# Opening of a fused two-block kernel: modulation rows loaded and summed whole, one group of four depth blocks multiplied in fp32 unsplit, two phases of 4 and 12 depth blocks, a short lead

## What is computed

```python
c_act = jax.nn.silu(c)                                  # c: 2048 values
mod = (c_act @ ada_w[i] + ada_b[i])[:, None, :]         # ada_w[i]: 2048 x 6144
shift, scale, gate = jnp.split(mod, 3, axis=-1)
h = rmsnorm(x, norm_g[i]) * (1.0 + scale) + shift
proj = h @ ret_w_in                                     # 2048 x 12288: q, k, v, g
```

## Time and profile before

| | us |
|---|---|
| three runs | 2258.05 (2257.55 to 2258.37) |
| the profiled execution | 2258.34 |
| its span | 2256.6 |
| TensorE busy | 2213.6 (98%) |
| DVE busy | 1489.8 (66%) |
| ACT busy | 1039.2 (46%) |
| mean granted clock of TensorE | 0.993 |
| HBM read | 498.04 MB, 222 GB/s over the span |

### The profile page before, as it was taken

How to read it: one execution, slowest core, us unless ns; L and a number is a source line. 1 busy time by engine, 2 the same in 40 slices (tenths; PEclk the granted TensorE clock), 3 DMA queues, 4 the chain that set the end, 5 groups by cost and what they waited for, 6 DMA issues and landing times.

```text
span 2256.6 us, 26895 instructions
## 1 busy us (share of the span) xinstructions
PE 2213.6 (98%) x10348; PEld 1835.5 (81%) x10348; DVE 1489.8 (66%) x1899; ACT 1039.2 (46%) x1353; POOL 101.7 (5%) x81
## 2 busy tenths in 40 slices
PE   5999999999999989999999999999999999999999
PEld 4878887878887778989888788878888888888887
DVE  7898778778876978655685555665555455555554
ACT  4544354443444445445455455454444344344343
POOL 0000000000000000000021200000100000000000
PEclk8999999999999999999999999999999999999999
DMA  9998577878887759735466454555566665666654
GB/s 349 374 329 300 169 265 270 308 251 311 286 299 249 280 200 338 247 109 173 148 188 218 155 177 139 167 190 187 185 189 186 195 187 186 196 186 189 194 186 141
DMA packets 139794, 501.91 MB, mean 222 GB/s; under 512 B 15633, under 2 KB 16145, under 8 KB 139153
## 3 DMA queue, kind: packets, MB, share of 16 engines
q1 hardware_dynamic: 139376, 499.99, 66.2%
q10 hardware_dynamic: 290, 0.21, 0.0%
HBM read 498.04 MB, written 2.10 MB: 222 GB/s over the span
## 4 chain that ended last, share of the span: by engine, by line
PE 88%; DVE 5%; DMA 3%; ACT 2%; issue 1%; POOL 1%; SPq 0%; DVEq 0%; ACTq 0%
PE ps L1008 72%; PE ps L1019 7%; PE ps L1080 2%; PE ps L1033 2%; DMA raw<-in_ret_in 2%; DVE wlo L1569 1%; ACT whi L1259 1%; DVE raw L1576 1%; DMA arena<-in_ret_in 1%; PE ps L1072 0%; DVE arena L1776 0%; PE ps L1177 0%; DVE x L1784 0%; POOL arena L1981 0%; DVE alo L1569 0%
## 5 line engine op out<-in xcount | busy, mean ns | idle before, releaser
L1569 DVE TENSOR_TENSOR wlo<-raw,whi 128x1024 fp32r<-128x1024 f32 (+1 forms) x711 | 867.9, 1226 | 575.9 <-ACT whi L1259 573.4
L1259 ACT ACTIVATE whi<-raw 128x1024 fp32r<-128x1024 f32 (+1 forms) x711 | 739.6, 1044 | 802.8 <-PE ps L1008 639.5
L1008 PE MATMUL ps<-whi,ahi 128*128 128x512 f32 x2482 | 789.3, 398 | 4.6 <-ACT whi L1259 1.7
L1008 PE MATMUL ps<-wlo,ahi 128*128 128x512 f32 x2482 | 771.8, 391 | 5.3 <-DVE wlo L1569 5.2
L1008 PE MATMUL ps<-whi,alo 128*128 128x512 f32 x2482 | 771.8, 391 | 0.0
L1008 PEld LDWEIGHTS ps<-wlo,ahi 128*128 128x128 f32 x2482 | 466.7, 188 | 107.2 <-DVE wlo L1569 8.2
L1008 PEld LDWEIGHTS ps<-whi,alo 128*128 128x128 f32 x2482 | 467.5, 188 | 98.9
L1008 PEld LDWEIGHTS ps<-whi,ahi 128*128 128x128 f32 x2482 | 457.0, 189 | 96.9 <-issue 3.8
L1576 DVE SCALAR_TENSOR_TENSOR raw<-raw,arena 128x1024 f32<-128x1024 f32 x184 | 223.9, 1218 | 0.0
L1019 PE MATMUL ps<-whi,ahi 128*128 128x512 f32 x254 | 99.6, 392 | 0.0
L1019 PE MATMUL ps<-wlo,ahi 128*128 128x512 f32 x254 | 98.9, 389 | 0.0
(11 more groups left out here) (209 smaller groups left out, 1343.8 us busy)
## 6 DMA issues: line engine op xcount, KB each, us to landing
raw<-in_mlp SPq DMA_DIRECT2D x256, 512.0 KB, 3.6
raw<-in_ret_in SPq DMA_DIRECT2D x188, 512.0 KB, 4.9
raw<-in_ada_t SPq DMA_DIRECT2D x184, 512.0 KB, 5.0
raw<-in_in SPq DMA_DIRECT2D x80, 512.0 KB, 4.3
raw<-in_ret_out SPq DMA_DIRECT2D x64, 512.0 KB, 4.9
raw<-in_mla_in SPq DMA_DIRECT2D x48, 512.0 KB, 4.6
raw<-in_mla_out SPq DMA_DIRECT2D x32, 512.0 KB, 4.2
raw<-in_out SPq DMA_DIRECT2D x32, 512.0 KB, 3.8
```

Of the source, the lines that this page charges most:

```text
L1008: mm = e.matmul(acc_[:, :], (ahi, alo, ahi)[m][:, slot, kb, tb * P:(tb + 1) * P], parts[m][:, chunk(n)], start=first and m == 0, stop=False)
L1259: e.activation(high(i)[:, 0:ncol], raw_of(n)[:, 0:ncol], ACT.Copy).then_inc(*s_hi.up(i))
L1569: e.tensor_tensor(low(i)[:, 0:ncol], raw_of(n)[:, 0:ncol], high(i)[:, 0:ncol].bitcast(F32), ALU.subtract).then_inc(*s_lo.up(i))
```

## The change

1. Ada rows: one load of 1 MB (2048 inputs, two neighbouring lanes) and one DVE instruction with its sum per tile, in place of two; `mods` and `gate_sum` lose the addition of the halves. The stored array is laid out so that a partition's row is 8 KB in one piece.
2. `DIRECT`: the four blocks with index 0, 2, 4, 6 (qk of depth blocks 0 to 3) aren't split. TensorE multiplies the raw fp32 weight by the modulated input in `scr`, one fp32 product in place of three. Their lanes are free when TensorE has used them.
3. Phases of 4 and 12 depth blocks. The rows of depth blocks 4 to 15 (24 loads of 1 MB) are strewn from index 8 to index 38. v next stays in PSUM from the first phase into the second.
4. `pump` emits loads as far ahead as before, but splits and sums (`make`) only two blocks ahead of TensorE until index 44, then seven as before.
5. Turns 0 to 3 come before the first block, turns 4 to 7 after index 8 and the next ones. The diagonal comes ahead of the first ada sums. The low part of h0 is made after the split of the v block of its depth block.
6. Gate rows and the second layer's rows are placed only after every second weight, so that pairs of lanes stay aligned.

```diff
-PHASES = [range(0, 4), range(4, 10), range(10, 16)]
+PHASES = [range(0, 4), range(4, 16)]
+BESIDE, LAZY = 8, 44
+DIRECT = range(0, BESIDE, 2)
-ORDERS = [("qk", "v", "g", "qk next", "v next"), ("v next", "qk next", "g", "v", "qk"),
-          ("qk", "v", "qk next", "v next", "g")]
+ORDERS = [("qk", "v", "g", "qk next", "v next"), ("v next", "qk", "v", "qk next", "g")]
...
-    for kbs, first_w, last_w in ((PHASES[1], 8, 30), (PHASES[2], 30, 60)):
-        for j in range(24):
-            due.setdefault(first_w + j * (last_w - first_w) // 24, []).append((kbs[j // 4], j // 2 % 2, j % 2))
+    for j in range(24):
+        due.setdefault(BESIDE + j * 16 // 24 * 2, []).append((PHASES[1][j // 2], j % 2))
...
+    def pump(upto, made=None):
+        while at["next"] < len(plan) and at["weight"] <= upto:
+            n = at["next"]
+            at["next"] += 1
+            do("load", n)
+            at["weight"] += plan[n][0] == "w"
+        if made is None:
+            made = upto if at["used"] > LAZY else min(upto, at["used"] + 2)
+        consume(made)
+    def make():
+        n = at["made"]
+        at["made"] += 1
+        if plan[n][0] == "w":
+            i = at["split"]
+            at["split"] += 1
+            if i not in DIRECT:
+                do("split", i, n)
+            if i < BESIDE and i % 2:
+                do("mod_low", range(i // 2, i // 2 + 1))
+            return
+        _, layer, kb, c = plan[n]
+        do("adt", layer, kb, c, n)
+        if c == 1 and layer == 0 and kb in PHASES[0]:
+            do("mods", layer, kb, 1)
+            if kb:
+                mod_begin(range(kb, kb + 1))
...
-    pump(0, 3)
+    pump(7, -1)
     do("norm_diag", "h0")
-    pump(0, 6)
+    for _ in range(2):
+        make()
     turn_first(0)
-    mod_to(0)
     turn_first(1)
+    mod_begin(range(1))
+    consume(1)
+    turn_first(2)
+    turn_first(3)
...
+            def direct(name, kb, i, got, first, end):
+                n = weights[i]
+                w.wait_ge(*s_raw[lanes[n]].on(n))
+                w.wait_ge(*s_act.on(("mod_first", kb)))
+                for c, tb in got:
+                    acc_ = empty(got[c, tb]) if first else ps[got[c, tb][0]]
+                    mm = e.matmul(acc_[:, :], scr[:, kb % 4 * 256 + tb * P:kb % 4 * 256 + (tb + 1) * P], raw_of(n)[:, chunk(c)], start=first, stop=end)
```

More of the change, by code:

```diff
@@ L176, in schedule @@
     side, urgent, ready, modulated = deque(), deque(), deque(), set()
-    at = {"next": 0, "weight": 0, "used": 0, "ahead": 0}
+    at = {"next": 0, "weight": 0, "made": 0, "split": 0, "used": 0, "ahead": 0}
     met = {}
@@ L193, in pump, with consume @@
             do("load", n)
[L194 to L209, removed]
+            at["weight"] += plan[n][0] == "w"
+        if made is None:
+            made = upto if at["used"] > LAZY else min(upto, at["used"] + 2)
+        consume(made)
+    def consume(upto):
+        while at["made"] < at["next"] and at["split"] <= upto:
+            make()
[16 more added lines that the diff above has]
+                mod_begin(range(kb, kb + 1))
+        elif c == 1 and kb % 2:
+            do("mods", layer, kb - 1, 2)
+            if layer == 0:
+                ready.append(range(kb - 1, kb + 1))
+        elif c == 2 and kb % 4 == 3:
+            do("gate_sum", layer, kb // 4)
+            urgent.append((at["used"] + 3, lambda layer=layer, j=kb // 4: gate_row(layer, j)))
     def gate_row(layer, j):
@@ L357, in side_by_side @@
                 w = next_block()
+                if w in DIRECT:
+                    do("direct", name, kb, w, got[name], begin, i == len(kbs) - 1)
+                elif i < len(kbs) - 1:
+                    do("block", 0, ("h0", kb), w, 1024, got[name], begin)
+                else:
+                    for key in got[name]:
+                        do("tail", ("first", name, moved[name]), 0, "h0", key, [(w, kb)], got[name][key], key == (1, 1))
                 if i < len(kbs) - 1:
[L359 to L362, removed]
                     step_jobs()
                     continue
-                for key in got[name]:
-                    do("tail", ("first", name, moved[name]), 0, "h0", key, [(w, kb)], got[name][key], key == (1, 1))
                 part_out(name, got.pop(name))
@@ L398, in schedule @@
         if ph == 0:
+            side += [lambda k2=k2: turn_first(k2) for k2 in range(4, 8)]
             do("later_in")
[L400 to L403, removed]
+        else:
+            side += [lambda: do("angles"), lambda: do("reduced"), lambda: do("tables")] + ropes(0) + qk_turns(0)
         for name in order[2:]:
-            one_group(name, kbs, held, ph < 2 and name == ORDERS[ph + 1][0])
-            if ph == 2 and name == "qk next":
+            one_group(name, kbs, held, ph == 0 and name == ORDERS[1][0])
+            if ph and name == "qk next":
                 side += ropes(1)
@@ L785, in xn, with lane_of @@
             return x[:, kb % 2, kb // 2 * 256:kb // 2 * 256 + 256]
[L788 to L792, removed]
-        def raw_of(n):
[L795 to L799, removed]
+        def lane_of(m):
+            return m % EARLY if m < 24 else (m - 24 + 24 % EARLY) % RAW
+        lanes, lanes_before, held_by = [], [], {}
+        at_lane = 0
+        for n, item in enumerate(plan):
+            size = 1 if item[0] == "w" else 2
+            at_lane += at_lane % size
+            own = [lane_of(at_lane + i) for i in range(size)]
+            lanes.append(own[0])
+            lanes_before.append(sorted({held_by[lane] for lane in own if lane in held_by}))
+            held_by.update((lane, n) for lane in own)
+            at_lane += size
+        def raw_of(n):
+            lane, width = lanes[n], 1024 if plan[n][0] == "w" else 2048
+            a = flat(raw) if lane < RAW else flat((dtab, sg, v, v_next)[(lane - RAW) // 2])
+            first = (lane if lane < RAW else (lane - RAW) % 2) * 1024
+            return a[:, first:first + width]
         R0 = Region()
@@ L940, in load @@
             def load(n):
[L941 to L944, removed]
-                    w.wait_ge(*s_lo.on(i))
-                elif m is not None:
-                    w.wait_ge(*s_ada.on(plan[m]))
+                for m in lanes_before[n]:
+                    if plan[m][0] != "w":
+                        w.wait_ge(*s_ada.on(plan[m]))
+                    elif weight_at[m] in DIRECT:
+                        w.wait_ge(*s_mm.on(("used", weight_at[m])))
+                    else:
+                        w.wait_ge(*s_hi.on(weight_at[m]))
+                        w.wait_ge(*s_lo.on(weight_at[m]))
                 landed = s_raw[lanes[n]]
@@ L1395, in v_copy @@
             def v_copy():
-                w.wait_ge(*s_vec.on(("part", LAST["v next"], "v next", 1, 1)))
+                w.wait_ge(*s_act.on(("part", LAST["v next"], "v next", 1, 1)))
                 w.wait_ge(*s_att.on(("ret_values", 0, 1, 1)))
```

76 lines of the change are left out of this document (42 added, 34 removed).

## The result

The changed kernel takes 2286.1 us (median of four runs, 2284.4 to 2289.2); the kernel before, beside it, 2257.8. The ratio is 1.0128, 95% interval 1.0112 to 1.0144: slower by 28 us, where 6 were forecast. The profiled execution has a span of 2283.9, 27.3 more than before.

What follows compares the result with a forecast made beforehand. TensorE's work bounds the kernel, busy 2213.6 of 2256.6 us, with supply close behind. Only the 6.2 us delay at index 38 counted: 2258.3 + 6.2 = 2264.5, median 2264; range 2250 to 2273.

Steps and rivals of the forecast that it cites:

- Parts 1 and 2: Opening: lazy splits, early turns and direct blocks end index 7 at 51.2 us instead of 66.8; direct blocks add 2.9.
- Nothing on the path: Opening: direct blocks' extra 2.9 us of TensorE work falls where it waits for rows anyway, so costs no time.
- The walk: Opening, traced step by step in the new order: each depth block costs DVE 8.7 us; index 7 ends at 51.2.
- Part 4: Index 8 to 38: 79 units of 512 KB at 1.42 us make supply the bound; index 38 starts 6.2 us later.
- Part 3: Whole rows: two DVE instructions of 1.14 us become one of 2.3, with no price on the path by itself.
- R1: Rival, lanes between index 8 and 38: whole rows reach 1.28 us a unit, 3.2 us earlier, 2255; chance 0.26.
- R3: Rival, opening supply: short lead and coarse lanes slow it to 1.55 us a unit, +15 us, 2273; chance 0.1.
- Under 340 GB/s: Sign of R3, 60 to 150 us: DMA rate under 340 GB/s, with ACT waiting for TensorE.
- DVE over 85% busy: Sign that the forecast is right, about 52 to 157 us: DVE over 85% busy, ACT's waits ended by landings.
- The rule of 1 MiB transfers: Ring loads: batching to 1 MiB or more for 75% of peak would raise the rate; a rival, not the forecast.
- Part 5: After index 38: each block needs one unit, 1.42 against 2.72 us, so TensorE sets the pace and nothing is added.
- if the time changes behind index 80: Sign against the forecast, late code: a change of time behind index 80 makes its account fall.

Runs made afterwards that it cites:

- run 4: The changed kernel without direct blocks, all eight first blocks split: 2286.0 us, 1.0131 of the kernel before.
- 7: The changed kernel with half rows and three phases; short lead and direct blocks kept: 2252.7 us, 0.9983 of the kernel before.
- 8: The changed kernel with half rows, three phases and no direct blocks; short lead kept: 2259.0 us, 1.0008 of the kernel before.
- run 1: The changed kernel with half rows (512 KB loads) again, the rest of the change kept: 2270.4 us, 1.0062 of the kernel before.
- run 3: The changed kernel with the long lead (seven blocks) from index 8 on: 2277.5 us, 1.0091 of the kernel before.
- run 13: run 1 with the short lead only up to index 8, the long lead after: 2269.8 us, 1.0061 of the kernel before.
- run 5: The changed kernel with each whole row fetched by two 512 KB loads, the whole sum kept: 2285.7 us, 1.0129 of the kernel before.
- 12: run 1 with the head turns four steps later: 2265.8 us, 1.0039 of the kernel before.
- 14: The changed kernel with the head turns four steps later: 2276.6 us, 1.0089 of the kernel before.
- run 10: run 1 with eight raw lanes in place of six until load 96: 2262.8 us, 1.0025 of the kernel before.
- run 11: Half rows, three phases, short lead and direct blocks (as 7) with eight lanes until load 72: 2248.5 us, 0.9963 of the kernel before.
- run 9: The changed kernel with eight raw lanes in place of six until load 96: 2267.2 us, 1.0053 of the kernel before.

## Why the prediction was wrong in size

- *Parts 1 and 2* (opening) held. Direct blocks were forecast at 18.8, 27.7, 36.4 and 45.1 and started at 18.54, 26.97, 35.41 and 43.84; index 7 was to end at 51.2 and did so at 52.0. The rows of the direct blocks are 3.67, 5.37, 3.67 and 5.37 us long, not 3.44: the granted clock was 0.66 in 27 to 32 us, after a hole of 2 us, and 1.00 in 36 to 40, after one of 0.3. The rows' pace covered it, as forecast. "Nothing on the path" is true of their cost, not of what they save: by run 4 some 3 us up to 340 us, by 7 against 8 six. The walk implied it and the sum never used it.
- *Part 4* (two phases denser) held within 1.5 us at index 38 with half rows. Taking 1.42 us a unit it put index 12 at 60.3 + 3 × 1.42 = 64.6 and the split of 38 at 155.4; run 1 shows 65.35 and 156.88, the changed kernel 64.37 and then 167.90. Run 1's time is still 14 us above the kernel before and not 6: 4.3 are the rotation, 1.4 the split of index 38, and 2.1 more come between 38 and 42, which take 13.0 us in place of 4 × 2.72.
- ***Part 3* is the step that failed**: "No price on the path by itself, but the DVE can't start until 1 MB has landed, and two lanes come free at once." The sentence names the mechanism and gives it no price. It cost 1.62 instead of 1.42 us a unit, 12.6 us over 64 units. Half rows give 15.7 us of time back (run 1): 9.8 by index 42, and in the profiles 5.3 in the late stretch, whose cause is open. A warning was there: six lanes a round, an issue to landing of 6.0 us under load and 2.3 for the sum give 8.3 / 6 = 1.38 a unit at best, with next to nothing left for late returns. It doesn't give 1.62 by itself: the 1 MB loads took a median 7.2 us to land, which no row of before shows. R1 used 2.3 + 2.56 + 2.3 = 7.2 us instead, with the fixed part of an *empty* queue; in a full ring the time to land contains the queue itself.
- *R3* was this mechanism, at 1.55 us a unit. Its chance of 0.1 was too low and its end of the range too near: at 1.62 its own formula gives 60.3 + 67 × 1.62 + 1.06 = 169.9, and the changed kernel has 167.90 + 1.06 = 169.0. The 1.55 was worked out from no row. It blamed the short lead too; run 3 gives the ring 1.59 without it, and run 13 finds no cost. As its mark it named ACT waiting for TensorE: ACT waited for landings. "Under 340 GB/s" came true, "DVE over 85% busy" didn't (78% in 60 to 180 us).
- *The rule of 1 MiB transfers* (Trainium skill, "DMA: Bandwidth & Descriptors", Bandwidth) would have raised the rate. Here it fell, from 356 to 332 GB/s in 60 to 180 us (runs 1 and changed), and run 5 shows that the size of a transfer hardly matters at this point. With eight lanes halves still move more (405 against 390). The measurement decides; the rule says nothing of how much of a ring one transfer holds. The fixed part of about 2 us that the prediction gives beside the rule stands in another section of that page, "Anatomy of one DMA — SWDGE (gpsimd) path", for loads issued by GpSimd; SyncE issues these.
- *Part 5* ("after index 38 nothing") missed 4.3 us at L1132: with one phase fewer the head turns come sooner after the rotation that feeds them, and TensorE waits for DVE. It lay outside the stretch that I walked. Runs 12 and 14 show it. The prediction also said that its account falls if the time changes behind index 80: 5.1 us did, and for these it has none.
- Added up against the forecast's span, 2256.6 + 6.2 = 2262.8: 13.4 us more at index 42 (180.76 against 167.4), 4.2 by the first scores (the rotation), −1.7 by 850, 5.1 behind; 21.0 together, and the span measured is 21.1 above. The last term is open but for the 1.8 us wait at L1857.

The range ended at 2273 since it took R3 at 1.55 us a unit. At 1.62 R3's sum gives 2258.3 + 19.6 = 2277.9; the other 8 us are the rotation and the late stretch, which no rival had.

## What to carry to other kernels

A ring of buffers has a round: time from issue to landing under load, plus the time that a landed load waits for its consumer, plus the consumer. Divided by the buffers it gives the time per load. Landing and consumer alone give only a floor: (5.6 + 1.2) / 6 = 1.13 us for run 1, where 1.43 was measured. The middle term is the slack. Before you call a larger load free, ask whether that slack (1.7 us with half rows) covers what the larger load adds to landing and sum (1.3 + 1.1 here). Merging two loads and two consumers halves the number of places in the ring, and here one more pair of lanes gave 19 us back. And test the parts of a bundle apart: short lead, turns first and direct blocks together were good for 4.4 us, and for 8 with more lanes, and were buried beneath the other two. When two medians agree, compare the profiles at a landmark before saying that a part does nothing: run 4's 3 us were hidden by a difference in a late stretch of equal code.

## What the runs showed of the hardware

- Landing takes longer in a full ring: 512 KB took a median 5.2 to 5.5 us with six lanes (run 1, 98 to 124 us; 6.0 in the kernel before) against 3.6 where the queue was nearly empty, and 5.8 to 6.4 with eight lanes (run 10), though more bytes moved (402 against 365 GB/s in that window). From run 1 to run 10 each landing got longer, and the kernel faster.
- The DVE sum over 2048 columns took 2.286 us and over 1024 columns 1.219. From start to start, where the next one follows at once, it is 2.21 us (107.83 to 110.04 in the changed kernel) and 1.14 (99.12 to 100.26 in run 1): merging two saves less than 0.1 us.
- The granted clock fell to 0.93 in 60 to 180 us where TensorE stood still for 2 to 3 us at a time, and was 1.00 in 60 to 132 us of run 11, without a hole, and of run 9, with none over 1.8 us. If the rest of the stretch ran at 2.4 GHz, that is 14% of it at 1.2 GHz, by estimate 8 us of matmul time. It wasn't the bound here, since supply was; but it shows up as busy time, which is why the page of the changed kernel shows only 9.7 us of more holes.
